# Float32 projections to r, k and v, replaced by three products of rounded parts

## The chip, the cores and the metric

The kernel runs on one core of a Trainium2 chip. The metric is the device time of one execution in microseconds, as the median over runs. TensorE (PE) multiplies matrices into PSUM, VectorE (DVE) and ScalarE (ACT) work on SBUF and PSUM, GpSimd (POOL) and SyncE (SP) here mostly issue DMAs. Each engine follows its own program in order; they meet at semaphores.

## The reference

Two layers of a streaming encoder run over 1024 prompt frames and 64 frames of a sample; with padding that is T = 1092 columns of 1024 features. Layer 1 starts with RWKV-7 time mixing. What matters here is its beginning:

```python
xr, xw, xk, xv, xa, xg = (x + xx * mu[n] for n in range(6))   # xx: the frame before minus this one
r = xr @ w_r
k = xk @ w_k
v = xv @ w_v
logw = -jax.nn.softplus(-(w0 + jnp.tanh(xw @ w1) @ w2).astype(f32)) - 0.5
a = jax.nn.sigmoid((a0 + (xa @ a1) @ a2).astype(f32))
g = jax.nn.sigmoid(xg @ g1) @ g2
...
xs = tuple(t.transpose(1, 0, 2, 3) for t in (r_h, w_h, k_h, v_h, kk, b_h))
S_fin, o = lax.scan(step, wkv_prev.astype(f32), xs)
```

r, k and v are products of 1024 x 1024 weights with 1088 frames each. They are stored by head pair and go into a recurrence over chunks of 64 frames. All data are float32.

## The kernel before, in words

Activations lie feature-major: 8 tiles of 128 features by 1092 columns. A *unit* is one tile of 128 output features: all eight k-tiles by three column groups of 364, so 24 products into three PSUM banks. Two sets of banks alternate (`read0`, `read1`). Weights come by SP in chunks of 512 KB, one to a unit, into four slots of `W`, three units ahead.

There are two forms of unit. `unit` (line 404) multiplies float32 operands as they are: 24 matmuls. `split_unit` (line 425) works on rounded parts. A weight chunk w has an upper part wh (w cast to the rounded type float32r) and a rest wl = w - wh, an activation x has xh and xl, and the unit sums wh xh + wh xl + wl xh: 72 matmuls (line 443). DVE makes wh by a cast and wl in place by a subtraction (`split_chunk`, lines 1477 and 1478); ACT makes xh by a copy that rounds (lines 1026 and 1031), DVE xl by a subtraction (lines 1493 and 1504). The rounded names (`H_r`, `B_r`, `W_r`, `TM_r`) are the same memory as `H`, `B`, `W`, `TM`. Nearly all large products have the split form already; r, k and v have the plain one.

At the start of layer 1, `H` holds the residual and stays in SBUF; `A` holds the normed input. For each of six mixtures ACT scales a tile into `TM` (`mix`, line 1228), and DVE adds the shifted tile into one of two blocks of `B` (tiles 0 to 7 and 8 to 15, line 1436). The order is w, a, g, r, k, v. The first three go through two small products each (`lora`, lines 735 to 754). Then PE runs 8 units for r and 8 for k (`dense8`, line 495). ACT copies each unit from PSUM into one of four staging tiles of `B` (line 1253), and POOL stores it to DRAM (`keep`).

v is computed in a loop over eight head pairs (PE line 766, ACT 1280, DVE 1798, POOL 2132). For each pair POOL has loaded r, k, w and a from DRAM (`load_pair`, line 2126). ACT scales and squares the key (1285, 1288), PE sums the squares over a head, runs the pair's v unit, and sums the bonus products (`sums`, line 457); ACT copies both results out (1312, 1315). DVE meanwhile forms the factors of the recurrence: a first step on `a` (1803), the product with k (1806), the bonus product, a scan and the final products (1829 to 1837). POOL stores v, the bonus sums and the factors, then loads the pair after the next. What follows is the recurrence, whose chunks POOL loads (`load_chunk`, line 2164, `double_chunk`, lines 2170 and 2171).

Of the kernel before, what the change touches and what calls it, by code (L numbers as in the profile page):

```python
# [139 lines left out]
def build_trunk(nc, I, O, stop=99):  # L140
    ctx = ExitStack()
    with ctx:
# [11 lines left out]
        with ExitStack() as rounded:  # L154
# [35 lines left out]
                 "down": (DWr[:, 0, :], DWr[:, 1, :])}  # L190
# [97 lines left out]
        def c3(ap):  # L288
            return ap.rearrange("p (c n) -> p c n", c=NCH)

        def pset(s):
            return ps[:, NCH * s:NCH * s + NCH, 0:CH]
# [19 lines left out]
                 "xn_ready", "xn_tmp", "xv0", "xv1", "xv2", "xv3", "xs0", "xs1", "xs2", "xs3", "key_sq", "rk_ready", "gn_in", "dev_sq",  # L312
# [84 lines left out]
        def _(pe):  # L397
# [598 lines left out]
        def _(act):  # L996
# [225 lines left out]
            def mix(n):  # L1222

                for kt in range(KT):
# [29 lines left out]

            def hidden(slot, rows, func):
# [15 lines left out]
            stage()  # L1271
            mix(2)
            stage()
            mix(3)
            stage()
# [4 lines left out]
            with t.loop(2, l_in0=2 * 64, l_in1=2 * 64, act_p=16, dve_p=8, mm_done=12, read0=6, read1=6, key_scaled=4,  # L1280
                        key_sq=4, key_max=4, key_log=4, xs0=16, xs1=16, xs2=16, xs3=16) as i:
                for u in range(4):
# [27 lines left out]
                    act.wait_ge(S[f"xs{u}"], t.val(f"xs{u}"))  # L1310
                    t.up(f"xs{u}", 16)
                    nc.scalar.activation(c3(B[:, 18 + u, :]), pset(s), ACT.Copy).then_inc(S[f"read{s}"], 1)
# [114 lines left out]
        def _(dve):  # L1427
# [344 lines left out]
            for order, n in enumerate((1, 4, 5, 0, 2, 3)):  # L1772
                b = order % 2
                if order >= 2:
                    dve.wait_ge(S["mm_done"], read_by[order - 2])
                for kt in range(KT):
                    j = t.n.get("xn_tmp", 0) % 2
                    dve.wait_ge(S["xn_tmp"], t.up("xn_tmp"))
                    stt(B[:, 8 * b + kt, 1:T], A[:, kt, 0:T - 1], vec[:, V["mu0"] + n, kt:kt + 1], TM[:, j, 1:T],
                        ALU.mult, ALU.add).then_inc(S["xn_ready"], 1)  # L1780
                    t.up("xn_ready")
            t.skip(43)
# [15 lines left out]
            with t.loop(2, l_in0=2 * 64, l_in1=2 * 64, act_p=16, dve_p=8, mm_done=12, read0=6, read1=6, dve_step=12,  # L1798
                        key_rn=4, key_scaled=4, rk_ready=4, rn_used=4, pair_stored=4, sum_stored=4, pair_done=4) as i:
                for u in range(4):  # L1800
# [3 lines left out]
                                                 kab[:, bass.ds(pair, 1)], ALU.mult, ALU.add))  # L1804
                    dve.wait_ge(S["key_scaled"], t.up("key_scaled"))
# [172 lines left out]
            for i in range(NPAIR):  # L1978
# [11 lines left out]
                nc.vector.tensor_tensor(out, dev, gate, ALU.mult).then_inc(S["gn_ready"], 1)  # L1990
            channel_mixer(1)
# [3 lines left out]
        def _(pool):  # L1995
# [101 lines left out]

            pool.wait_ge(S["shift_in"], 1)
# [19 lines left out]
            for name in "rk":  # L2118
                keep(name)
# [12 lines left out]
            for i in range(NPAIR):  # L2132
# [3 lines left out]
                j = i % 4  # L2136
                pool.dma_start(d_v[i, :, 0:SEQ], B[:, 18 + j, P0:P0 + SEQ]).then_inc(S[f"xv{j}"], 16)
                pool.dma_start(d_v[i, :, SEQ:SEQ + C], B[:, 18 + j, S0:T]).then_inc(S[f"xs{j}"], 16)
                t.up(f"xs{j}", 16)
# [12 lines left out]
            for j in range(4):  # L2152
                pool.wait_ge(S[f"xs{j}"], t.val(f"xs{j}"))
                pool.wait_ge(S[f"xv{j}"], 32)
# [199 lines left out]
```

## Time and profile before

| what | us |
|---|---|
| runs: median of 3 (lowest, highest) | 4127.3 (4125.62, 4127.95) |
| profiled execution: its time | 4123.89 |
| profiled execution: its span | 4122.3 |
| PE busy in it | 3726.8 (90%) |
| DVE busy, ACT busy | 1461.3, 831.4 |

The span runs from the first to the last instruction of the one execution that was profiled; the profile's times count from its start. A row of a timeline merges like instructions and gives the idle time of the engine before them with what released it. A float32 matmul leaves two records, a rounded one one.

### The profile page before, as it was taken

How to read it: one execution, taken by the hardware profiler on the slowest of the kernel's cores; microseconds unless marked ns; L12 is line 12 of the kernel's file. 1: busy time of each engine (PE TensorE's matmuls, PEld its weight loads, DVE VectorE, ACT ScalarE, POOL GpSimd, SP SyncE). 2: the span in 40 equal slices, each digit the busy share in tenths (PEclk: the TensorE clock that was granted, in tenths of full speed). 3: DMA queues.
4: the chain of work that ended last, by engine and by line, in shares of the span. 5: the costliest groups of instructions: out<-in, count | busy, mean ns of one | idle time of the engine just before them, and what ended most of it. 6: DMA issues, size and time to landing. Idle time of an engine off the chain costs nothing.

```text
span 4122.3 us, 64833 instructions
## 1 busy us (share of the span) xinstructions
PE 3726.8 (90%) x27922; PEld 3201.6 (78%) x27922; DVE 1461.3 (35%) x1951; ACT 831.4 (20%) x1107; POOL 203.2 (5%) x345
## 2 busy tenths in 40 slices
PE   7998899899999998878998868889797999999977
PEld 4996337789999998754564537878496999999967
DVE  3123544342212223432211645555635222222352
ACT  2000232210000001223311423333322000000021
POOL 0001000000000000000000211111100000000000
PEclk9998999999999999986999989999999999999989
DMA  2212002111121131002222652211311112112211
GB/s 87 73 53 85 21 21 76 70 45 41 46 83 48 46 124 47 29 21 107 96 74 103 258 187 54 53 45 52 139 42 69 46 36 73 62 46 87 77 37 69
DMA packets 75064, 291.43 MB, mean 71 GB/s; under 512 B 9368, under 2 KB 11688, under 8 KB 71128
## 3 DMA queue, kind: packets, MB, share of 16 engines
q0 software_dynamic: 36528, 165.56, 11.1%
q1 hardware_dynamic: 38336, 122.87, 9.6%
q8 instruction: 167, 2.74, 0.3%
q14 instruction: 33, 0.27, 0.0%
HBM read 211.77 MB, written 76.62 MB: 70 GB/s over the span
## 4 chain that ended last, share of the span: by engine, by line
PE 72%; DVE 8%; ACT 2%; issue 2%; DMA 1%; POOL 0%; DVEq 0%; ACTq 0%; POOLq 0%
PE ps L443 47%; PE ps L417 11%; DVE A L1436 2%; PE ps L836 2%; PE ps L845 2%; DVE B L1436 1%; PE ps L750 1%; PE ps L457 1%; DVE H L1517 1%; PE ps L796 1%; DVE A_r L1493 1%; PE ps L475 1%; DVE B L1900 1%; PE ps L859 1%; PE ps L823 1%
## 5 line engine op out<-in xcount | busy, mean ns | idle before, releaser
L443 PE MATMUL ps<-A_r,TM_r 128*128 128x364 f32 x2736 | 605.3, 329 | 0.0
L443 PE MATMUL ps<-H_r,W_r 128*128 128x364 f32 (+1 forms) x2616 | 576.3, 328 | 0.0
L443 PE MATMUL ps<-H_r,TM_r 128*128 128x364 f32 x2352 | 520.8, 329 | 19.0 <-DVE A_r L1493 19.0
L417 PE MATMUL ps<-B,W 128*128 128x364 f32 (+1 forms) x1488 | 469.7, 477 | 24.9 <-DVE B L1436 24.9
L443 PEld LDWEIGHTS ps<-A_r,TM_r 128*128 128x128 f32 x2736 | 476.0, 189 | 0.0
L443 PEld LDWEIGHTS ps<-H_r,W_r 128*128 128x128 f32 (+1 forms) x2616 | 453.5, 187 | 1.8
L417 PEld LDWEIGHTS ps<-B,W 128*128 128x128 f32 (+1 forms) x1488 | 282.5, 190 | 207.6 <-issue 28.7
L443 PEld LDWEIGHTS ps<-H_r,TM_r 128*128 128x128 f32 x2352 | 408.0, 188 | 23.7 <-issue 14.5
L443 PE MATMUL ps<-B_r,DW_r 128*128 128x364 f32 x2112 | 408.8, 329 | 0.0
L443 PE MATMUL ps<-B_r,W_r 128*128 128x364 f32 x1824 | 404.6, 330 | 0.0
L443 PEld LDWEIGHTS ps<-B_r,DW_r 128*128 128x128 f32 x2112 | 358.8, 188 | 0.0
L443 PEld LDWEIGHTS ps<-B_r,W_r 128*128 128x128 f32 x1824 | 319.3, 189 | 0.0
L1695 DVE TENSOR_TENSOR TM<-ps,TM 128x1092 f32<-128x1092 f32 x44 | 57.0, 1296 | 444.1 <-PE ps L443 444.1
L1477 DVE CAST TM_r<-W 128x1024 fp32r<-128x1024 f32 x114 | 78.7, 690 | 321.7 <-PE ps L443 301.9
L443 PE MATMUL ps<-B_r 128*128 128x364 f32 x768 | 152.2, 334 | 14.3 <-DVE B_r L1504 14.3
L1169 ACT ACTIVATE B_r<-TM 128x1092 f32 (+1 forms) x44 | 49.2, 1118 | 542.6 <-DVEq L1697 542.6
L475 PE MATMUL ps<-TM,cst 128*128 128x364 f32 x288 | 107.9, 533 | 55.0 <-ACT TM L1004 55.0
L443 PEld LDWEIGHTS ps<-B_r 128*128 128x128 f32 x768 | 133.8, 192 | 15.5 <-issue 15.5
L1436 DVE SCALAR_TENSOR_TENSOR B<-A,vec,TM 128x1091 f32<-128x1091 f32 x48 | 62.9, 1352 | 225.0 <-ACT TM L1228 224.9
L1478 DVE TENSOR_TENSOR W_r<-W,TM_r 128x1024 fp32r<-128x1024 f32 x114 | 139.7, 1226 | 3.9
L475 PEld LDWEIGHTS ps<-TM,cst 128*128 128x128 f32 x288 | 60.3, 216 | 103.9 <-issue 65.9
L836 PE MATMUL ps<-B 64*64 64x64 f32 x2720 | 116.3, 224 | 25.9 <-issue 12.0
(279 smaller groups left out, 4146.4 us busy)
## 6 DMA issues: line engine op xcount, KB each, us to landing
W<-in_wgu SPq DMA_DIRECT2D x88, 512.0 KB, 3.6
W<-in_wdown SPq DMA_DIRECT2D x32, 384.0 KB, 3.1
W<-in_wrkv SPq DMA_DIRECT2D x24, 512.0 KB, 3.7
W<-in_wdown SPq DMA_DIRECT2D x32, 320.0 KB, 2.9
d_h<-H POOLq DMA_DIRECT2D x16, 546.0 KB, 3.0
d_y<-TM POOLq DMA_DIRECT2D x16, 546.0 KB, 3.6
A<-d_y POOLq DMA_DIRECT2D x16, 546.0 KB, 7.8
H<-d_h POOLq DMA_DIRECT2D x2, 4368.0 KB, 22.7
```

Source lines behind the costliest of these rows:

```text
L417: ins = nc.tensor.matmul(ps[0:cols, NCH * s + c, 0:CH], W[0:rows, slot, j * cols:(j + 1) * cols], xs[n][0:rows, c * CH:(c + 1) * CH], star ...
L443: ins = nc.tensor.matmul(ps[0:cols, NCH * s + c, 0:CH], w[:, j * cols:(j + 1) * cols], x[k1][:, c * CH:(c + 1) * CH], start=(k1 == 0 and n ...
L457: ins = nc.tensor.matmul(ps[:, NCH * s + c, 0:CH], lhs, x[:, c * CH:(c + 1) * CH], start=True, stop=True)
L475: ins = nc.tensor.matmul(ps[:, NCH * s + c, 0:CH], k("ones"), TM[:, j % 2, c * CH:(c + 1) * CH], start=(j == 0), stop=(j == KT - 1))
L750: ins = nc.tensor.matmul(ps[:, NCH * s + c, 0:CH], W[0:rows, slot, m * P:(m + 1) * P], out[0:rows, c * CH:(c + 1) * CH], start=True, stop= ...
L836: ins = nc.tensor.matmul(ps[r, g, C * a:C * a + C], AB[c % 2][r, p, :], Ms[c % 2][r, p, :], start=True, stop=True)
L845: ins = nc.tensor.matmul(ps[r, g, 256 + C * a:256 + C * a + C], MT[r, p, :], Y[r, p, :], start=True, stop=True)
L1169: nc.scalar.activation(hi, TM[:, j, :], ACT.Copy).then_inc(S["mid_hi"], 1)
L1436: return nc.vector.scalar_tensor_tensor(out=out, in0=in0, scalar=scalar, in1=in1, op0=op0, op1=op1)
L1477: step(nc.vector.tensor_copy(wh, w))
L1478: nc.vector.tensor_tensor(Wr[:, slot, 0:n], w, wh, ALU.subtract).then_inc(S["wl_ready"], 1)
L1695: nc.vector.tensor_tensor(c3(TM[:, j, :]), pset(s), c3(TM[:, j, :]), ALU.mult).then_inc(S[f"read{s}"], 1)
```

## The change

The 24 units of r, k and v become split units. The upper parts of the mixtures go into `H_r`, that is, into the residual's memory. POOL therefore stores the residual to DRAM as soon as it is complete (`d_h`, semaphore `hs_out`), and loads it back in the first chunks of the recurrence (`hs_in`). The rests xl stay in the mixture's block of `B`.

There is one `H_r` for three mixtures: the upper part of the next is written after PE's last unit on the one before. Weights are split by DVE (`split_weights`), each chunk at the earliest when the unit before the last has ended; upper parts of weights alternate between two tiles (of `TM` for r and k, of `B` for v). Since two of the four staging tiles hold those of v, the copies of r, k and v alternate between two tiles. In the loop over pairs DVE splits one chunk per pair.

```diff
-                 "down": (DWr[:, 0, :], DWr[:, 1, :])}
+                 "down": (DWr[:, 0, :], DWr[:, 1, :]),
+                 "rkv": (TMr[:, 2, 0:KT * P], TMr[:, 3, 0:KT * P]),
+                 "value": (Br[:, 20, 0:KT * P], Br[:, 21, 0:KT * P])}
...
+            xh = [Hr[:, j, :] for j in range(KT)]
+            xlow = [[Br[:, 8 * b + j, :] for j in range(KT)] for b in range(2)]
+            enter(t, "rkv")
             for n in range(2):
-                pe.wait_ge(S["xn_ready"], t.up("xn_ready", KT))
-                xs = X[(n + 1) % 2]
-                dense8(KT)
-
-            pe.wait_ge(S["xn_ready"], t.up("xn_ready", KT))
-            xs = X[1]
-            with t.loop(2, mm_done=12, read0=6, read1=6, key_sq=4, rk_ready=4, chunk=4, w_used=4, w0=16, w1=16, w2=16, w3=16):
+                t.up("xn_ready", KT)
+                split_units(KT, xh, xlow[(n + 1) % 2])
+
+            t.up("xn_ready", KT)
+            enter(t, "value")
+            pe.wait_ge(S["xl_ready"], t.up("xl_ready", KT))
+            with t.loop(2, mm_done=12, read0=6, read1=6, key_sq=4, rk_ready=4, chunk=4, w_used=4, w0=16, w1=16, w2=16, w3=16,
+                        wl_ready=4, wh=4):
                 for u in range(4):
                     pe.wait_ge(S["key_sq"], t.up("key_sq"))
                     sums(k("pair"), TM[:, 1, :])
-                    unit([KT], xs)
+                    split_unit(xh, xlow[1])
                     pe.wait_ge(S["rk_ready"], t.up("rk_ready"))
                     sums(k("pair"), TM[:, 2, :])
 
...
+
+            def staged(n, bufs):
+
+                j = n % bufs
+                s, mm, rd = t.unit()
+                act.wait_ge(S["mm_done"], mm)
+                act.wait_ge(S[f"xs{j}"], t.val(f"xs{j}"))
+                t.up(f"xs{j}", 16)
+                nc.scalar.activation(c3(B[:, 18 + j, :]), pset(s), ACT.Copy).then_inc(S[f"read{s}"], 1)
+
+            def upper_mixed(b, kt):
+
+                act.wait_ge(S["xn_ready"], t.val("xn_tmp", kt + 1 - KT))
...
             mix(0)
-            stage()
+            act.wait_ge(S["hs_out"], 16)
+            for n in range(KT):
+                staged(n, 4)
+                upper_mixed(1, n)
             mix(2)
-            stage()
-            mix(3)
-            stage()
+            for n in range(KT):
+                staged(n, 2)
+            for n in range(KT):
+                upper_mixed(0, n)
+            for n in range(KT):
+                if n < 2:
+                    mix(3, 4 * n, 4 * n + 4)
+                staged(n, 2)
+            for n in range(KT):
+                upper_mixed(1, n)
 
 
             log_and_exp()
             act.wait_ge(S["xn_ready"], t.val("xn_tmp"))
             with t.loop(2, l_in0=2 * 64, l_in1=2 * 64, act_p=16, dve_p=8, mm_done=12, read0=6, read1=6, key_scaled=4,
...
-                    nc.scalar.activation(c3(B[:, 18 + u, :]), pset(s), ACT.Copy).then_inc(S[f"read{s}"], 1)
+                    act.wait_ge(S[f"xs{u % 2}"], t.val(f"xs{u % 2}"))
+                    t.up(f"xs{u % 2}", 32)
+                    nc.scalar.activation(c3(B[:, 18 + u % 2, :]), pset(s), ACT.Copy).then_inc(S[f"read{s}"], 1)
...
-            for order, n in enumerate((1, 4, 5, 0, 2, 3)):
-                b = order % 2
-                if order >= 2:
+            def mix(order, n, k0=0, k1=KT):
+
...
+
+                for kt in range(KT):
+                    dve.wait_ge(S["xh_ready"], t.up("xh_ready"))
+                    nc.vector.tensor_tensor(Br[:, 8 * b + kt, :], B[:, 8 * b + kt, :], Hr[:, kt, :],
+                                            ALU.subtract).then_inc(S["xl_ready"], 1)
+                    t.up("xl_ready")
+
+            def split_weights(done):
+
+                slot, landed = t.chunk()
+                if done:
+                    dve.wait_ge(S["mm_done"], done)
+                dve.wait_ge(S[f"w{slot}"], landed)
+                w, wh = W[:, slot, 0:KT * P], wh_of(t)
+                step(nc.vector.tensor_copy(wh, w))
+                nc.vector.tensor_tensor(Wr[:, slot, 0:KT * P], w, wh, ALU.subtract).then_inc(S["wl_ready"], 1)
+                t.up("wl_ready")
+
+            t.n["chunk"] = t.n["w0"] = t.n["w1"] = t.n["w2"] = t.n["w3"] = 0
+            t.skip_chunks(CHUNKS[1] - 4 * KT)
+            enter(t, "rkv")
+            mix(0, 1)
+            mix(1, 4)
+            mix(2, 5)
+            mix(3, 0)
+            split_weights(0)
+            lower_mixed(1)
+            split_weights(0)
+            mix(4, 2)
+            for m in range(2, KT + 1):
+                split_weights(mm0 + 27 + m - 1)
+            lower_mixed(0)
+            split_weights(mm0 + 27 + KT)
+            dve.wait_ge(S["mm_done"], read_by[3])
+            step(nc.vector.memset(B[:, 8:16, 0:1], 0.0))
+            mix(5, 3, 0, 4)
+            split_weights(mm0 + 27 + KT + 1)
+            mix(5, 3, 4, 8)
+            for m in range(KT + 3, 2 * KT):
+                split_weights(mm0 + 27 + m - 1)
+            enter(t, "value")
+            dve.wait_ge(S["xs2"], 96)
+            dve.wait_ge(S["xs3"], 96)
+            lower_mixed(1)
...
                 for u in range(4):
                     pair, key, L = i * 4 + u, key2[u % 2], Lb[u % 2]
                     dve.wait_ge(S[f"l_in{u % 2}"], t.up(f"l_in{u % 2}", 64))
                     step(nc.vector.tensor_scalar(tmpA, L["a"], vec[:, V["ka"], bass.ds(pair, 1)],
                                                  kab[:, bass.ds(pair, 1)], ALU.mult, ALU.add))
+                    split_weights(0)
                     dve.wait_ge(S["key_scaled"], t.up("key_scaled"))
...
+            dve.wait_ge(S["hs_in"], 16)
             channel_mixer(1)
...
+            pool.wait_ge(S["h_ready"], 24)
+            pool.dma_start(d_h, H[:, :, :]).then_inc(S["hs_out"], 16)
             pool.wait_ge(S["shift_in"], 1)
...
+            pool.wait_ge(S["hs_out"], 16)
+            pool.dma_start(H[:, :, :], d_h).then_inc(S["hs_in"], 16)
             with t.loop(3, u_done=8, tok_done=8, zi0=96, zi1=96) as i:
```

Left out: counts in the loops' headers, and POOL's stores of r, k and v, which go over two staging tiles instead of four.

DVE from the mixture of w to the loop over pairs, before (1436: six mixtures of eight tiles; the memsets prepare the scan):

```order
L1436 SCALAR_TENSOR_TENSOR B<-A,vec,TM 128x1091 x48
L1786 MEMSET B 128x1092
L1787 MEMSET B 128x16
L1788 MEMSET B 128x1
L111 UNCONDITIONAL_BRANCH
```

and the same place now, up to the third weight chunk of r (1466: mixtures; 1828, 1829: `split_weights`; 1817: `lower_mixed`):

```order
L1466 SCALAR_TENSOR_TENSOR B<-A,vec,TM 128x1091 x32
L1828 CAST TM_r<-W 128x1024
L1829 TENSOR_TENSOR W_r<-W,TM_r 128x1024
L1817 TENSOR_TENSOR B_r<-B,H_r 128x1092 x8
L1828 CAST TM_r<-W 128x1024
L1829 TENSOR_TENSOR W_r<-W,TM_r 128x1024
L1466 SCALAR_TENSOR_TENSOR B<-A,vec,TM 128x1091 x8
L1828 CAST TM_r<-W 128x1024
```

The mixtures no longer stand in one run: after those of w, a, g and r come the first weights and the rests of r, then the mixture of k, and from there a pair of splitting instructions for each unit.

ACT now, from r's mixture to the loop over pairs (1234: `mix`; 1268: `staged`, a copy out of PSUM; 1273: `upper_mixed`); the copy and the upper part before the "..." stand eight times in turn:

```order
L1234 ACTIVATE TM<-A,mub 128x1092 x8
L1268 ACTIVATE B<-ps 128x1092
L1273 ACTIVATE H_r<-B 128x1092
...
L1234 ACTIVATE TM<-A,mub 128x1092 x8
L1268 ACTIVATE B<-ps 128x1092 x8
L1273 ACTIVATE H_r<-B 128x1092 x8
L1234 ACTIVATE TM<-A,mub 128x1092 x4
L1268 ACTIVATE B<-ps 128x1092
L1234 ACTIVATE TM<-A,mub 128x1092 x4
L1268 ACTIVATE B<-ps 128x1092 x7
L1273 ACTIVATE H_r<-B 128x1092 x8
```

Before, only mixtures and copies alternated here. Upper parts of r stand between the copies of g; those of k stand behind the last copy of r, those of v behind the last copy of k.

DVE at the start of a pair, before:

```order
L1803 TENSOR_SCALAR A<-B,vec,kab 128x1092
L1433 ISA
L1805 REGISTER_ALU
L1806 TENSOR_TENSOR B<-A,B 128x1092
L1433 REGISTER_ALU
```

and now (1880 is 1803, 1884 is 1806):

```order
L1880 TENSOR_SCALAR A<-B,vec,kab 128x1092
L1463 ISA
L1826 REGISTER_ALU
L1828 CAST B_r<-W 128x1024
L1463 REGISTER_ALU
L1829 TENSOR_TENSOR W_r<-W,B_r 128x1024
L1883 REGISTER_ALU
L1884 TENSOR_TENSOR B<-A,B 128x1092
```

The cast and the subtraction stand between the pair's first step and the product that waits for ACT's scaled key.

## Rows read from the trace of the kernel before

**Rows 1.** Page, head: the whole profiled execution.

```profile
span 4122.3 us, 64833 instructions
```

**Rows 2.** Stretch table of the r and k units: busy per engine, clock, DMA share.

```profile
1990.96:2226.00 235.04, 235.04 (x769) 145.73 (x767) 20.97 (x16) 36.12 (x32) 9.05 (x17) 1.00 0.22 78
```

**Rows 3.** Chain of waits, one rounded unit: start us, us, what.

```profile
1690.24 11.95 PE ps L443 x72
```

**Rows 4.** PE's timeline, g units to v units: start us, us, what, [idle before <-releaser].

```profile
1977.51 13.62 PE L750 MATMUL ps<-B,W 128*128 128x364 f32 x36 [7.34 <-ACT B L1253]
...
1990.96 235.04 PE L417 MATMUL ps<-B,W 128*128 128x364 f32 x768
...
2243.52 4.00 PE L457 MATMUL ps<-TM,cst 128*128 128x364 f32 x6 [17.52 <-ACT TM L1288]
...
2315.57 2.86 PE L457 MATMUL ps<-TM,cst 128*128 128x364 f32 x6 [3.48 <-ACT TM L1288]
...
2318.23 15.82 PE L417 MATMUL ps<-B,W 128*128 128x364 f32 x48
...
2408.96 3.76 PE L457 MATMUL ps<-TM,cst 128*128 128x364 f32 x6 [3.48 <-ACT TM L1288]
```

**Rows 5.** Splitting instructions by line: min/median/max ns, first and last start.

```profile
L1031 ACT ACTIVATE B_r<-B x16: 1096/1098/1113, 689.7 to 2999.4; 128x1092 fp32r<-128x1092 f32 x16
...
L1477 DVE CAST TM_r<-W x114: 685/690/695, 58.3 to 4072.7; 128x1024 fp32r<-128x1024 f32 x114
...
L1478 DVE TENSOR_TENSOR W_r<-W,TM_r x114: 1224/1226/1228, 59.0 to 4073.4; 128x1024 fp32r<-128x1024 f32 x114
...
L1504 DVE TENSOR_TENSOR B_r<-B,B_r x16: 1285/1289/1291, 691.6 to 3002.5; 128x1092 fp32r<-128x1092 f32 x16
```

**Rows 6.** PE's timeline after the longer idle before the output projection.

```profile
2995.53 2.16 PE L443 MATMUL ps<-B_r 128*128 128x364 f32 x6 [10.18 <-DVE B_r L1504]
...
3000.36 1.16 PE L443 MATMUL ps<-B_r 128*128 128x364 f32 x6
...
3001.86 1.16 PE L443 MATMUL ps<-B_r 128*128 128x364 f32 x6
```

**Rows 7.** ACT's timeline around the g units.

```profile
1976.39 2.03 ACT L1253 ACTIVATE B<-ps 128x1092 f32<-128x1092 f32 x2
...
1981.55 1.08 ACT L1253 ACTIVATE B<-ps 128x1092 f32<-128x1092 f32 x1 [3.13 <-PE ps L750]
```

**Rows 8.** ACT's timeline from the last k unit to the first pair.

```profile
2226.04 1.08 ACT L1253 ACTIVATE B<-ps 128x1092 f32<-128x1092 f32 x1 [13.60 <-PE ps L417]
...
2241.04 1.21 ACT L1285 ACTIVATE A<-B,vec 128x1092 f32<-128x1092 f32 x1 [12.62 <-DMA B<-d_a]
```

**Rows 9.** DVE's timeline in one pair of the v loop.

```profile
2314.33 1.29 DVE L1806 TENSOR_TENSOR B<-A,B 128x1092 f32<-128x1092 f32 x1 [4.70 <-ACT A L1285]
...
2316.85 1.35 DVE L1436 SCALAR_TENSOR_TENSOR TM<-B,vec 128x1092 f32<-128x1092 f32 x1 [1.23 <-POOLq L2144]
...
2330.24 1.35 DVE L1436 SCALAR_TENSOR_TENSOR A<-A,B 128x1024 f32<-128x1024 f32 x2
...
2332.35 0.85 DVE L1803 TENSOR_SCALAR A<-B,vec,kab 128x1092 f32<-128x1092 f32 x1 [0.75 <-DMA B<-d_a]
```

**Rows 10.** Stretch table of single pairs of the v loop.

```profile
2314.60:2338.30 23.70, 20.30 (x60) 12.12 (x60) 16.11 (x17) 10.84 (x13) 4.77 (x9) 0.93 0.68 258
...
2385.90:2408.00 22.10, 18.62 (x60) 11.32 (x60) 16.19 (x17) 11.01 (x13) 4.76 (x9) 1.00 0.72 276
```

**Rows 11.** POOL's DMA issues for the next pair, by line.

```profile
L2126 POOL DMA_DIRECT2D B<-d_a x8: 528/528/531, 2233.8 to 2391.5; - x8
```

**Rows 12.** Page, DMA issues: the residual's load: KB each, us to landing.

```profile
H<-d_h POOLq DMA_DIRECT2D x2, 4368.0 KB, 22.7
```

**Rows 13.** POOL's timeline at the start of the recurrence.

```profile
2484.75 0.62 POOL L2171 COPY B<-B 128x512 f32<-128x512 f32 x1
...
2515.32 0.88 POOL L2164 DMA_DIRECT2D B<-d_bk  x1 [5.87 <-PE ps L823]
```

More of the change, by code:

```diff
@@ L311, in build_trunk @@
                  "pt_done", "pt_read", "o_done", "o_read", "ot_done", "ot_read", "bias_in0", "bias_in1", "kv_in0", "kv_in1", "attn_pair",
[L312 removed]
+                 "xn_ready", "xn_tmp", "hs_out", "hs_in", "xs0", "xs1", "xs2", "xs3", "key_sq", "rk_ready", "gn_in", "dev_sq",
                  "b_out", "key_scaled", "sum_out", "pair_done", "pair_stored", "sum_stored", "rn_used", "key_max", "key_log", "key_rn", "l_in0", "l_in1", "gn_in0", "gn_in1", "mean_in", "gn_used", "shift_in", "conv_out",
@@ L1220, in _, with mix @@
             act.wait_ge(S["dve_p"], t.up("dve_p"))
-            def mix(n):
-                for kt in range(KT):
+            def mix(n, k0=0, k1=KT):
+                for kt in range(k0, k1):
                     j = t.n.get("xn_tmp", 0) % 2
@@ L1253, in stage @@
                         nc.scalar.activation(c3(B[:, 18 + j, :]), pset(s), func, **kw).then_inc(S[f"read{s}"], 1)
+            def staged(n, bufs):
[7 more added lines that the diff above has]
+                act.wait_ge(S["xn_ready"], t.val("xn_tmp", kt + 1 - KT))
+                nc.scalar.activation(Hr[:, kt, :], B[:, 8 * b + kt, :], ACT.Copy).then_inc(S["xh_ready"], 1)
             def hidden(slot, rows, func):
@@ L1280, in _ @@
             with t.loop(2, l_in0=2 * 64, l_in1=2 * 64, act_p=16, dve_p=8, mm_done=12, read0=6, read1=6, key_scaled=4,
-                        key_sq=4, key_max=4, key_log=4, xs0=16, xs1=16, xs2=16, xs3=16) as i:
+                        key_sq=4, key_max=4, key_log=4, xs0=64, xs1=64) as i:
                 for u in range(4):
@@ L1771, in _ @@
             dve.wait_ge(S["dve_step"], t.up("dve_step"))
-            for order, n in enumerate((1, 4, 5, 0, 2, 3)):
-                b = order % 2
-                if order >= 2:
+            def mix(order, n, k0=0, k1=KT):
+                if order >= 2 and k0 == 0:
                     dve.wait_ge(S["mm_done"], read_by[order - 2])
-                for kt in range(KT):
+                for kt in range(k0, k1):
                     j = t.n.get("xn_tmp", 0) % 2
                     dve.wait_ge(S["xn_tmp"], t.up("xn_tmp"))
-                    stt(B[:, 8 * b + kt, 1:T], A[:, kt, 0:T - 1], vec[:, V["mu0"] + n, kt:kt + 1], TM[:, j, 1:T],
+                    stt(B[:, 8 * (order % 2) + kt, 1:T], A[:, kt, 0:T - 1], vec[:, V["mu0"] + n, kt:kt + 1], TM[:, j, 1:T],
@@ L1780, in _, with lower_mixed @@
                         ALU.mult, ALU.add).then_inc(S["xn_ready"], 1)
                     t.up("xn_ready")
+            def lower_mixed(b):
+                for kt in range(KT):
[12 more added lines that the diff above has]
+                t.up("wl_ready")
@@ L1796, in tokens @@
                 return ap[:, P0:P0 + SEQ].rearrange("p (c n) -> p c n", n=C), ap[:, S0:T]
-            with t.loop(2, l_in0=2 * 64, l_in1=2 * 64, act_p=16, dve_p=8, mm_done=12, read0=6, read1=6, dve_step=12,
-                        key_rn=4, key_scaled=4, rk_ready=4, rn_used=4, pair_stored=4, sum_stored=4, pair_done=4) as i:
+            with t.loop(2, l_in0=2 * 64, l_in1=2 * 64, act_p=16, dve_p=8, mm_done=12, read0=6, read1=6, dve_step=16,
+                        key_rn=4, key_scaled=4, rk_ready=4, rn_used=4, pair_stored=4, sum_stored=4, pair_done=4,
+                        chunk=4, w0=16, w1=16, w2=16, w3=16, wl_ready=4, wh=4) as i:
                 for u in range(4):
@@ L2118, in _ @@
             for name in "rk":
-                keep(name)
+                with t.loop(4, mm_done=2, read0=1, read1=1, xs0=16, xs1=16) as i:
+                    for j in range(2):
+                        s, mm, rd = t.unit()
+                        pool.wait_ge(S[f"read{s}"], rd)
+                        pool.sem_inc(S["held"], 1)
+                        pool.dma_start(d_x[name][bass.ds(i * 2 + j, 1)].rearrange("a p n -> (a p) n"),
+                                       B[:, 18 + j, :]).then_inc(S[f"xs{j}"], 16)
+                        t.up(f"xs{j}", 16)
             for j in range(4):
@@ L2135, in _ @@
                 pool.wait_ge(S[f"read{s}"], rd)
-                j = i % 4
-                pool.dma_start(d_v[i, :, 0:SEQ], B[:, 18 + j, P0:P0 + SEQ]).then_inc(S[f"xv{j}"], 16)
+                j = i % 2
+                pool.dma_start(d_v[i, :, 0:SEQ], B[:, 18 + j, P0:P0 + SEQ]).then_inc(S[f"xs{j}"], 16)
                 pool.dma_start(d_v[i, :, SEQ:SEQ + C], B[:, 18 + j, S0:T]).then_inc(S[f"xs{j}"], 16)
-                t.up(f"xs{j}", 16)
+                t.up(f"xs{j}", 32)
                 s, mm, rd = t.unit()
```

3 lines of the change are left out of this document (removed).

## The prediction

> **What bounds the kernel now.** I read the head of the page first: a span of 4122.3 us [rows 1]. The profiled execution took 4123.9 us, so 1.6 us lie outside the span; the median of the runs shown is 4127.3, 3.4 us above it. The sum is made against 4123.9, and 3.4 is added at the end.
>
> Then I looked for what the change touches. The stretch table shows that PE was busy for all of the 235.04 us of the r and k units, at a granted clock of 1.00, the 2.4 GHz level, while DVE worked for 20.97 us and ACT for 36.12 [rows 2]. PE alone bounds this stretch, and DVE has room. PE's timeline gives its content: 768 records, two to a float32 matmul, so 384 matmuls in 16 units of 24; 235.04 / 16 = 14.69 us a unit, 612 ns a matmul [rows 4]. The chain of waits has the price of the other form in the same kernel: a unit of 72 rounded matmuls takes 11.95 us, 166 ns each [rows 3]. That unit is the one at line 443, with the same 128x364 shape. Three products for 498 ns stand against one for 612.
>
> The v units stand in a loop over eight head pairs. A pair there is a serial ring: PE's sum (2.86 us), PE's unit (15.82 with some time at the lower clock level), PE's second sum, two ACT steps, and PE's next sum, before which PE sat idle 3.48 us for ACT [rows 4]. From the first sum at 2243.52 to the eighth at 2408.96 are seven pairs of 23.63 us.
>
> **The change part by part.** *Units.* 24 units fall from 14.69 to 11.95, 2.74 us each: 16 x 2.74 = 43.8 us for r and k, which stand back to back on PE, and 8 x 2.74 = 21.9 us for v, if the ring closes no sooner elsewhere.
>
> By the Trainium skill (TensorE: Matmul & The Clock Gate, "Wait — 56ns, not 53.3ns?") warm matmuls follow each other after their columns at 2.4 GHz plus about 2.5 ns. For 364 columns that is an estimate of 154 ns, a unit of 11.1 us, and 20 us more gain over 24 units, so about 4048. The trace does not agree for this form, 166 ns in [rows 3], and the measurement decides; the sum stays with 11.95.
>
> *Start of r.* ACT now makes one upper part (1.10 us, line 1031 [rows 5]) between two copies of g units (1.08 [rows 7]), 2.18 us a unit. Its third g copy started at 1981.55, after a wait for PE [rows 7]; two copies and two uppers from 1976.39 end at 1980.75, so this start stands. The seventh copy then starts at 1981.55 + 4 x 2.18 = 1990.3 and ends at 1991.4; it frees the PSUM set of the first r unit, which began at 1990.96 [rows 4]. Cost 0.6 us. The k-tiles of r come every 2.18 us from long before, the last at about 1996, and PE asks for its eighth some 10 us after its start. Bounds: nothing, and 4.9 us if PE had to wait for all eight; I take 0.6.
>
> *From r to k.* There is one block for upper parts, so k's cannot be written until PE has ended the last r unit. PE then waits for ACT's copy (1.08 [rows 7]), the first upper (1.10) and the first subtraction (1.29 [rows 5]), and three hand-overs. One is about 0.13 us: the sum of a pair began at 2315.57 [rows 4], 1.24 after the ACT step before it, which takes about 1.1 like line 1031's and starts when line 1806 does, at 2314.33 [rows 9]. So 3.47 + 0.4 = 3.9 us. Further tiles come each 1.29 us, faster than the 1.50 that PE takes for nine matmuls [rows 6]. After an idle PE starts at the lower clock level: after 10.18 us idle two tiles took 4.83 us instead of 3.0, 1.8 lost [rows 6]; in the v loop, idle 3.48 us, a pair takes 23.7 us at a mean clock of 0.93, and one at 1.00 took 22.1, so 1.6 lost [rows 10]. The second idle is nearer in length: 1.6. Bounds 0 and 1.8. Together 5.5 us.
>
> *Supply of weights.* Each unit asks DVE for a cast (0.69) and a subtraction (1.23 [rows 5]), 1.92 us of 11.95, made a unit ahead; 16 x 1.92 + 16 x 1.29 of new work beside 20.97 in some 198 us. It is hidden by PE's units. The thinnest cover is the second k unit: its weights are split behind eight subtractions of k, that is 2.5 + 8 x 1.29 + 1.92 = 14.7 us after the end of r, and the first k unit ends at 3.9 + 1.6 + 11.95 = 17.5. Without these 2.8 us PE waits by what is missing.
>
> *From k to v.* PE sat idle 17.52 us here already [rows 4], for the store of the last k tile and the loads of the first pair, which ended ACT's wait of 12.62 us at 2241.04 [rows 8]. The eight uppers of v start after the copy at 2226.04 + 1.08 and end 8 x 1.10 later, 2235.9; the last subtraction ends at 2237.2. The table load and the memset that stand there still fit. Cost 0.
>
> *The v loop.* DVE gets 1.92 us, put between its first step on a pair (line 1803) and the product at line 1806. Counted from 1806 at 2314.33: the last products end at 2331.59, +17.3; 1803 waited 0.75 for the pair's load and began at +18.0 [rows 9]. With 0.85 for it and 1.92 for the split DVE is ready at +20.8 to +21.0. The ring closes at 23.63 - 2.74 = 20.89. That is level; but the next step waited 1.23 us for POOL's store of the bonus sums in any case [rows 9], so DVE may be a microsecond late for nothing. ACT asks for the load 1.2 us before 1806, at +19.7, and it landed at +18.0. Both covers shrink to 1 to 2 us; none is gone. I take the whole 21.9. From the other side: if the clock came back, DVE's own round of 17.3 + 0.85 + 1.92 = 20.0 us is the floor, 8 x 3.6 = 29 us. At worst the loop keeps its 23.63 and gains nothing.
>
> The casts meet a rule of the Trainium skill (SBUF — State Buffer, "SBUF: two separate sides"): a VectorE copy in a two-port mode locks GpSimd out and holds up the descriptors of DMAs that it issues. POOL issues this loop's stores and loads; its issue took 528 to 531 ns in all eight pairs [rows 11], with no cast beside it. By the rule a cast of 0.69 could hold each pair's chain once, 5.5 us in all, 4074 instead of 4068; it runs 2 us or more away from the loads, so I leave it out.
>
> *The residual.* Its store is issued before layer 1's norm, and the two first lora products lie between it and its first need. The reload takes 22.7 us [rows 12]. POOL reaches it after the copy at 2484.75, so it would end at 2508.1, in the old time; the queue's next load came at 2515.32 [rows 13]. Cost 0; if nothing hid it, 22.7.
>
> *Sum:* -43.8 + 0.6 + 5.5 - 21.9 = -59.6 us; 4123.9 - 59.6 = 4064.3; with 3.4, **4068 us** for the median.
>
> **The rivals.** *A new bound in the loop.* The load of the pair or DVE's round takes the place of PE's unit. For it: the DMA engines were 0.68 busy in a pair [rows 10], and the same bytes in 20.9 us make 0.77, so the load may land later than +18.0; beyond +19.7 each microsecond is a microsecond of the period. Against: stores and loads start from the same event as before, so they keep their places to each other. The loop would gain between 0 and about 13 us: 4077 to 4090.
>
> *More than the sum.* The idle before k does not lower the clock, and the loop's clock recovers, so that DVE's 20.0 us is the period: -1.6 and -7 more, 4059; if the first k tile also came without ACT's copy in front, 4055.
>
> *Slower: the clock in the rounded units.* The changed program has one idle more, at k, and the loop's idle of 3.48 us stands in a shorter pair. If the granted clock stayed at 1.2 GHz for a share f of the 24 units, each such unit would take 23.9 us. The gain is gone at 24 x 11.95 x f = 59, f = 0.21, and the kernel is 0.2% slower from f = 0.24; at f = 0.3 it is 4154. Against: the r and k units ran at 1.00 although an idle of 7.34 us stood shortly before [rows 4], and the rounded units of [rows 3] hold 166 ns, possible only at 2.4 GHz.
>
> *It does not do what it says:* the units cost PE as much as before (operands that are written shortly before could be read slower), and only the 6 us of gaps come in: about 4134, no change.
>
> **How the numbers follow.** The measurement tells apart about 0.2%, 8 us. Forecast: 0.70, own range 4060 to 4077. New bound in the loop: 0.17, 4077 to 4090. More: 0.07, 4047 to 4060. No effect: 0.03. Slower: 0.03. So faster 0.94, same 0.03, slower 0.03. The range reaches into both neighbours, 4055 to 4088.
>
> **What would show it.** Right: 16 runs of 72 rounded matmuls at 11.95 to 12.0 us; one idle of about 4 us between the eighth and ninth; PE's idle before the first pair still near 17.5; periods of 20.9 in the loop, with 1803 still waiting for the load and 1806 for ACT or hardly at all. Wrong: idles before units ended by DVE's subtraction of weights; periods above 21.5 with ACT waiting for the pair's load; a granted clock under 0.95 in the r and k stretch; PE waiting at the start of the recurrence for POOL's copies.

## The result and the profile after

The changed kernel takes 4101.9 us in the median (4098.2 to 4107.4) against 4127.3: a ratio of 0.9935, 95% interval 0.9922 to 0.9948. It is faster, by 25 us where 59 were forecast, and lies outside the range given. The profiled execution is the longest of its three, 4107.4 us.

First the page's head, then the stretch table (from:to, us, busy us and instructions of PE, PE's weight loads, DVE, ACT and POOL, granted clock, DMA share, GB/s) for r and k. They answer [rows 1, 2].

```profile
span 4105.5 us, 66070 instructions
```

```profile
1991.65:2087.41 95.76, 95.75 (x576) 95.44 (x575) 28.23 (x27) 19.62 (x18) 4.80 (x9) 1.00 0.30 101
2090.99:2188.51 97.52, 97.50 (x576) 97.20 (x576) 31.98 (x30) 22.28 (x21) 3.73 (x7) 0.98 0.25 87
```

The span fell by 16.8 us. The sixteen units are there as forecast: 95.76 / 8 = 11.97 us each for r. The chain of waits (start us, us, what) shows the hand-over from r to k, and PE's timeline (start us, us, what, [idle before <-releaser]) the loop over head pairs and the start of the recurrence; they answer [rows 3, 4].

```profile
1991.65 95.76 PE ps L445 x576
...
2087.43 1.08 ACT B L1268
2088.52 1.01 ACT H_r L1273
...
2089.55 1.31 DVE B_r L1817
...
2090.99 97.52 PE ps L445 x576
```

```profile
1978.03 13.62 PE L752 MATMUL ps<-B,W 128*128 128x364 f32 x36 [7.34 <-ACT B L1268]
1991.40 0.76 PE L445 MATMUL ps<-H_r,TM_r 128*128 128x364 f32 x3
...
2206.21 4.00 PE L459 MATMUL ps<-TM,cst 128*128 128x364 f32 x6 [17.71 <-ACT TM L1318]
...
2355.49 4.00 PE L459 MATMUL ps<-TM,cst 128*128 128x364 f32 x6 [3.48 <-ACT TM L1318]
...
2401.10 6.98 PE L533 MATMUL ps<-cst 128*128 128x512 f32 x10 [26.75 <-POOL B L2258]
```

The last row is the five matmuls (ten records) that raise the clock ahead of the recurrence. They began at 2457.41 in the kernel before and begin at 2401.10 now: 56.3 us of the 59.6 are there at this point. The same table over the recurrence, from these matmuls to the eleven of the same kind behind it, shows where they go: the kernel before, then the changed one.

```profile
2457.40:2911.50 454.10, 393.88 (x10155) 358.35 (x10155) 239.48 (x540) 163.04 (x400) 67.95 (x93) 0.96 0.18 48
```

```profile
2401.10:2890.60 489.50, 413.37 (x10155) 374.91 (x10155) 241.85 (x540) 161.98 (x400) 68.99 (x95) 0.91 0.19 54
```

The same 10,155 matmul records take 35.4 us more: 19.5 us of PE's busy time, at a granted clock of 0.91 instead of 0.96, and 15.9 us of idle (60.2 to 76.1). Behind the recurrence another 4.1 us are lost, and -56.3 + 35.4 + 4.1 = -16.8. No line of PE's code in the recurrence was touched. What PE waits for there (line <- releaser: us in all, times, longest), before and after:

```profile
PE ps L796 <- DVE B L1900: 24.7, 16, 2.5
PE ps L836 <- issue: 12.0, 10, 3.7
```

```profile
PE ps L842 <- issue: 27.5, 12, 3.5
...
PE ps L901 <- issue: 9.9, 4, 2.8
PE ps L802 <- DVE B L1978: 7.8, 8, 2.5
```

(Lines 796 and 836 of before are 802 and 842 now.) "Issue" is a wait for nothing that the profile shows. It has taken the place of the wait for DVE. Of the 12.0 us before, 7.2 stand at the two jumps back of PE's loop; there the changed kernel loses 6.5 of its 27.5, so the rest has grown from 4.8 to 21.0. PE's timeline shows where one stands, first before, then after:

```profile
2521.09 0.66 PE L845 MATMUL ps<-TM 64*64 64x64 f32 x16
2523.27 1.16 PE L796 MATMUL ps<-B 64*128 64x128 f32 x16 [1.52 <-DVE B L1900]
```

```profile
2463.78 0.41 PE L842 MATMUL ps<-B 64*64 64x64 f32 x6
2466.52 0.56 PE L842 MATMUL ps<-B 64*64 64x64 f32 x10 [2.32 <-issue]
...
2467.53 2.08 PE L802 MATMUL ps<-B 64*128 64x128 f32 x16
```

PE stops after six of a group's sixteen records, that is inside its eight float32 matmuls, whose waits all stand ahead of the first. So it lacks no operand; what it lacks is instructions, as the packets show below. The stop swallows the wait for DVE, and the next matmuls run at the lower clock level (2.08 us for what takes 1.16). The page has a DMA queue named instruction, 173 packets of 16,384 bytes; in this stretch PE's next packet began 2463.86 in the trace, 7.5 us after the last at 2456.40, where 4 to 6 us are common. POOL's loads for a later chunk stand in between. Its timeline, and the DMA view of 2457.8 to 2465.8 (busy tenths and GB/s in 40 slices, then the queues: packets, MB, share):

```profile
2458.29 0.89 POOL L2251 DMA_DIRECT2D B<-d_bk  x1 [5.85 <-PE ps L829]
...
2460.05 0.88 POOL L2251 DMA_DIRECT2D B<-d_v  x1
```

```profile
DMA  0000000000599537989999999999999998632010
GB/s 0 0 0 0 0 0 0 0 0 0 82 143 123 82 123 205 389 348 451 348 307 287 287 307 287 287 287 287 287 307 348 266 266 205 143 62 41 0 20 0
...
q0 software_dynamic: 364, 1.30, 59.9%
q8 instruction: 1, 0.02, 1.0%
```

The DMA engines are full from about 2461 to 2464.5, and the one packet of instructions comes at the end of that. By its record in the trace it has landed at 2465.09, and PE goes on 1.43 us later, at 2466.52.

That holds for nearly every such stop. Take the idle of PE, jumps back left out, that ends with no releaser, from 20 us into the recurrence on. In the changed kernel it is 46.3 us, and 45.2 of them end 1.1 to 1.8 us behind the landing of an instruction packet; in the kernel before it is 10.1 us, 7.9 of them behind a packet. Both kernels take 87 packets in the recurrence, one for 117 records of matmuls. Their number has not changed, only what PE has to wait for at them.

### The profile page after: what moved, and what is told of

Its sections match the earlier page's. It is cut to its first block, busy times and chain, and to the rows that moved or that the text cites. A ratio compares the mean times of both kernels' runs of the same rounds, so it can differ in the third digit from the quotient of the medians.

```text
span 4105.5 us, 66070 instructions
## 1 busy us (share of the span) xinstructions
PE 3695.8 (90%) x28498; PEld 3297.6 (80%) x28498; DVE 1538.2 (37%) x2024; ACT 853.8 (21%) x1131; POOL 207.6 (5%) x347
## 4 chain that ended last, share of the span: by engine, by line
PE 72%; DVE 7%; issue 2%; ACT 2%; DMA 1%; POOL 0%; DVEq 0%; ACTq 0%; POOLq 0%
PE ps L445 54%; PE ps L419 3%; DVE A L1466 2%; PE ps L851 2%; PE ps L842 2%; PE ps L459 1%; PE ps L752 1%; DVE B L1466 1%; PE ps L802 1%; DVE H L1547 1%; DVE A_r L1523 1%; PE ps L891 1%; PE ps L477 1%; PE ps L868 1%; PE ps L865 1%
## 5 line engine op out<-in xcount | busy, mean ns | idle before, releaser
L445 PE MATMUL ps<-H_r,W_r 128*128 128x364 f32 (+1 forms) x3192 | 704.9, 329 | 0.0
L445 PE MATMUL ps<-H_r,TM_r 128*128 128x364 f32 x2736 | 606.5, 330 | 21.7 <-DVE A_r L1523 18.1
L445 PEld LDWEIGHTS ps<-H_r,W_r 128*128 128x128 f32 (+1 forms) x3192 | 555.4, 188 | 1.8
L445 PEld LDWEIGHTS ps<-H_r,TM_r 128*128 128x128 f32 x2736 | 475.5, 189 | 26.5 <-issue 18.3
L445 PE MATMUL ps<-B_r 128*128 128x364 f32 x960 | 196.2, 335 | 13.9 <-DVE B_r L1534 13.9
L445 PE MATMUL ps<-B_r,TM_r 128*128 128x364 f32 x768 | 176.5, 338 | 17.9 <-DVE A_r L1523 17.9
L445 PEld LDWEIGHTS ps<-B_r 128*128 128x128 f32 x960 | 169.0, 194 | 15.1 <-issue 15.1
L445 PEld LDWEIGHTS ps<-B_r,TM_r 128*128 128x128 f32 x768 | 135.1, 191 | 24.7 <-issue 13.8
L842 PE MATMUL ps<-B 64*64 64x64 f32 x2720 | 116.8, 226 | 39.2 <-issue 27.5
L1952 DVE COPY_PREDICATED B<-lvl,ps 128x256 f32<-128x256 uint8 x170 | 75.3, 443 | 178.8 <-PE ps L851 177.9
```

Source lines behind the costliest of these rows:

```text
L445: ins = nc.tensor.matmul(ps[0:cols, NCH * s + c, 0:CH], w[:, j * cols:(j + 1) * cols], x[k1][:, c * CH:(c + 1) * CH], start=(k1 == 0 and n ...
L842: ins = nc.tensor.matmul(ps[r, g, C * a:C * a + C], AB[c % 2][r, p, :], Ms[c % 2][r, p, :], start=True, stop=True)
L1952: nc.vector.copy_predicated(Ms[c % 2][:, 4 * g:4 * g + 4, :], four(lvl[:, l + 1, :]), half_of(g, 256)).then_inc(S["m_ready"], 1)
```

## The theories

*A, the place of the code.* PE's instructions arrive in packets. The change puts 1440 more rounded and 288 fewer float32 matmuls into PE's code ahead of the recurrence (a loop's body counts once). With two and four instructions each, and 2 others, that is 2880 - 1152 + 2 = 1730 more, 194 above a multiple of 256, the number of instructions that theory A takes for a packet. So the seams between packets fall on other matmuls of every chunk. A1: a seam is dear where its packet is asked for beside POOL's loads and no wait of PE covers it. A2: a packet takes its time whatever else moves. *B, the residual's reload* disturbs the recurrence. *C, the clock* falls there by itself. *D,* the new code costs it in some other way.

## Experiments on the place of the code

The padding is one line ahead of the wait in which PE sat idle for 26.75 us:

```diff
+            for _ in range(62):
+                pe.sem_inc(S["held"], 1)
             pe.wait_ge(S["st_ready"], 1)
```

Expected of 62:

> The changed kernel with 62 semaphore increments on PE ahead of the recurrence, in the 26.75 us in which PE waits there for POOL. Theory A (place of the code): the change put some 1730 more instructions on PE ahead of the recurrence, which is 194 above a multiple of 256; PE's instructions come in packets of 16,384 bytes, one for every 121 or so matmul records, so the seams between packets lie at other matmuls of each chunk than before, and PE now stops there for 2 us in each of 17 chunks. 62 more bring the seams back to where they were: the recurrence, from the matmuls that raise the clock to the first store of the state, 486.8 us now, goes back to 452 to 456, and the kernel to 4066 to 4073. Theory B (the residual's reload disturbs the recurrence): nothing changes, 4098 to 4107. Theory C (the clock falls in the recurrence by itself, because of what ran before): nothing changes, 4098 to 4107.

Of 256, 128, 94, 190 and 30:

> A control for the padding: 256 semaphore increments at the same place, still inside PE's wait of 26.75 us. Theory A: the seams lie as in the changed kernel without padding, so the recurrence takes 484 to 489 us and the kernel 4098 to 4107. If padding of any length helped (by delaying PE, or by what it does to the clock), it would fall to 4066 to 4073 as with 62. Theories B and C: 4098 to 4107.

> 128 semaphore increments at the same place: half a packet, some 61 matmul records. Theory A: the seams lie at a third place; they go past more of a chunk's matmuls, so the time of the recurrence is neither bound to 487 nor to 453, I expect 445 to 490 and say only that it moves by more than 5 us against the changed kernel without padding (4066 to 4095 for the kernel). Theories B and C: 4098 to 4107.

> 94 semaphore increments ahead of the recurrence, between the place that gave 4070 (62) and the one that gave 4093 (128). Theory A, no more than that a seam's place decides: between 4065 and 4095, and stops of PE at a line that differs from those of 62 and of 128. Theories B and C would have it at 4098 to 4107.

> 190 semaphore increments on PE ahead of the recurrence: 30.0 us at 158 ns, 3.3 us more than PE's wait there, so a start 3 us late. The seams lie some 30 matmul records later than in the changed kernel without padding, if 256 instructions are one packet. Theory A: between 4070 and 4105, with stops at other lines than 842. If the seams repeat every 256 instructions, the time lies between those of 128 (4093) and 256 (4101, of which 14 are its late start), so 4085 to 4100.

> 30 semaphore increments: the seams lie some 15 matmul records earlier in a chunk than without padding, half way to the place that 62 gave. Theory A: between 4070 and 4102, I say 4086; stops still in line 842's groups in part of the chunks. Theories B and C: 4098 to 4107.

Measured (medians of four runs, of ten for 190 and three for none; ratio to the kernel before, run beside it, with its 95% interval; recurrence and PE busy from the stretch table as above; the last column has the idle behind instruction packets, counted as above, and how many of these stops are longer than 1 us):

| padding | median us | ratio | recurrence us | PE busy in it | stops us (over 1 us) |
|---|---|---|---|---|---|
| 0 | 4101.9 | 0.9935 (0.9922 to 0.9948) | 489.5 | 413.4 | 45.2 (17) |
| 30 | 4097.7 | 0.9933 (0.9915 to 0.9952) | 474.7 | 404.9 | 22.3 (5) |
| 62 | 4070.2 | 0.9859 (0.9842 to 0.9876) | 451.1 | 392.2 | 6.3 (2) |
| 94 | 4079.7 | 0.9886 (0.9869 to 0.9902) | 461.8 | 398.3 | 11.9 (3) |
| 128 | 4092.8 | 0.9916 (0.9899 to 0.9933) | 479.2 | 402.5 | 23.3 (5) |
| 190 | 4122.4 | 0.9989 (0.9978 to 1.0000) | 499.3 | 419.9 | 27.4 (10) |
| 256 | 4100.7 | 0.9942 (0.9925 to 0.9959) | 469.1 | 401.6 | 32.8 (13) |

Idle instructions, 62 of them, bring back 32 us, and 190 of them eat nearly all that the change had won. With 62 the waits of the recurrence read as those of the kernel before:

```profile
PE ps L802 <- DVE B L1980: 25.0, 16, 2.5
PE ps L842 <- issue: 11.2, 8, 3.8
```

With 190 the stops stand at other lines:

```profile
PE ps L533 <- issue: 30.6, 1, 30.6
PE ps L851 <- issue: 17.0, 12, 3.0
...
PE ps L802 <- issue: 14.6, 8, 3.4
```

B and C fall as the cause of these 32 us: neither has a reason why a few increments in an idle wait should matter. With 30, half way to 62 in the code, the time stays near that of none: no halving of the way halves the loss. The last column does not put the recurrences in order by itself: 190 has fewer stops than 0 and the longest recurrence, with the most PE busy time, at a granted clock of 0.91.

Three expectations were missed. With 94, PE's longest waits were to stand at a line other than with 62; they stand at line 842 in both (14.5 us with 94). The time with 190 was to lie between 4085 and 4100: I had drawn a line between two neighbours, and the curve has no such line, since what decides is which group of matmuls the seam cuts. The first row above shows that its increments outlasted the wait, 30.6 us against 26.75. The control with 256 has its stops at lines 842 and 901 as without padding, one of them on the very record of the 2.32 us stop above:

```profile
2475.85 0.41 PE L842 MATMUL ps<-B 64*64 64x64 f32 x6
2478.58 0.75 PE L842 MATMUL ps<-B 64*64 64x64 f32 x10 [2.32 <-issue]
```

So 256 increments move the seams by a whole packet. It has the total of the kernel without padding too, but by two errors that cancel: its increments took 40.6 us, which starts the recurrence 13.9 us late, and the recurrence took 469.1 us, not 484 to 489. The seams' place gives the place of the stops; what they cost at one place still differs between versions (469 to 490 us). The medians say so too: without its late start 256 would be 11 to 15 us faster than 0. Why stays open.

The other direction, in the kernel before, with 194 of the same increments:

> The kernel before, its r, k and v units untouched, with 194 semaphore increments on PE ahead of the recurrence, which puts the seams between the packets of PE's instructions where they lie in the changed kernel. One increment took 158 ns in the run with 256 (40.6 us in all), so 194 take 30.7 us, 2.5 us more than PE's wait of 28.18 there. Theory A (place of the code): PE now stops in the middle of line 836's 16 matmuls, as the changed kernel does at line 842, and the recurrence goes from 454 to between 469 and 490 us (what the runs with the same seams took); the kernel to 4145 to 4165 (454 to 469 or 490, and 2.5). Theory D (the stops come from the new code itself, its reload or its split units): 4125 to 4132, 2.5 us from the late start and nothing else.

It took 4148.2 us, ratio 1.0046 (1.0030 to 1.0062), slower by 18, of which 2.9 are the late start (31.1 us against 28.2). The recurrence took 470.6 us instead of 454.1, with old units and no reload. Its waits:

```profile
PE ps L531 <- issue: 31.1, 1, 31.1
PE ps L836 <- issue: 28.3, 14, 4.7
...
PE ps L895 <- issue: 6.2, 3, 2.4
PE ps L796 <- DVE B L1902: 5.7, 7, 2.5
```

The stops stand at the lines (836, 895) that are 842 and 901 in the changed kernel, and at the same record:

```profile
2528.22 0.41 PE L836 MATMUL ps<-B 64*64 64x64 f32 x6
2530.68 0.59 PE L836 MATMUL ps<-B 64*64 64x64 f32 x10 [2.04 <-issue]
```

(The sixteen in the expectation are records, of eight matmuls.) The stops behind packets grow from 7.9 us to 31.7. D falls as the cause of the stops: they need none of the new code. In size this run shows 16.5 of the 35.4 us, as the changed kernel does with the same seams at 256 (15.0).

## Experiments on the loads and the reload

Smaller loads:

```diff
-                    pool.dma_start(dst, src.rearrange("a p n -> p a n")[:, :, cols]).then_inc(S[f"zi{c % 2}"], 16)
+                    pool.dma_start(dst[:, 0:pairs, :], src.rearrange("a p n -> p a n")[:, 0:pairs, cols]).then_inc(S[f"zi{c % 2}"], 16)
...
-                    load_chunk(c + 3, at + 3)
+                    load_chunk(c + 3, at + 3, NPAIR if c == 0 else 1)
```

> The changed kernel, no padding, with the chunk loads of POOL in the recurrence cut to one head pair of eight, in three of four chunks; what it leaves out is the data of seven pairs in those chunks. PE's code is the same. Theory A1 (at the bad seams the packet of instructions waits behind POOL's loads on the DMA engines): the stops of 2 us at line 842 go in the chunks with small loads, the recurrence falls from 486.8 to 450 to 462, and the kernel to 4066 to 4080. Theory A2 (a packet takes its time whatever else the DMA engines do; it is only where the seam lies that counts): the stops stay, the recurrence at 469 to 490, the kernel at 4085 to 4105.

Measured: 4077.1 us, ratio 0.9880 (0.9864 to 0.9897); the recurrence 457.5. One run holds both cases. PE's timeline at the same place of two neighbouring chunks, then POOL's loads of the two, full ones (0.90 us to issue) and small ones (0.56):

```profile
2572.45 0.56 PE L842 MATMUL ps<-B 64*64 64x64 f32 x10 [2.04 <-issue]
...
2599.03 1.16 PE L802 MATMUL ps<-B 64*128 64x128 f32 x16 [1.31 <-DVE B L1978]
```

```profile
2564.64 0.90 POOL L2251 DMA_DIRECT2D B<-d_bk  x1 [5.72 <-PE ps L829]
...
2591.00 0.56 POOL L2251 DMA_DIRECT2D B<-d_bk  x1 [5.46 <-PE ps L829]
```

Behind full loads PE stops after six of sixteen records as in the changed kernel; behind small ones, with the same code, it does not stop, and waits for DVE as in the kernel before. The other chunks agree: after six records of line 842 PE stops for 0.89, 2.04 and 1.16 us in the three chunks of the loop with full loads, and from there on no stop behind a packet is over 0.8 us elsewhere. (The longest behind a packet, 4.05 us, stands ahead of them, beside the reload.) Then the full loads, only later:

```diff
+                    for _ in range(14):
+                        pool.sem_inc(S["held"], 1)
                     load_chunk(c + 3, at + 3)
```

> The changed kernel, no padding on PE (its seams stay at the bad place), with 14 semaphore increments on POOL between its wait for the token-major products and the three loads of a chunk: some 2.2 us at the 158 ns that one took on PE. The loads are wanted a chunk later, so PE does not wait for them. Theory A1 (a packet of instructions that PE asks for just behind the loads waits for them): the packet that stops line 842 now, wanted some 5 us after the one at 2456.40 and begun only at 2463.86, goes ahead of the loads' bytes; the stops at line 842 go in most chunks and the kernel comes to 4066 to 4085. Theory A2 (the seam's place alone): 4092 to 4105.

> The same with 30 increments, some 4.7 us. Theory A1: the packet of line 842 is free, but the next one, some 5 us later, now stands behind the loads; whether that stops PE depends on whether a wait for DVE covers it: stops at a line that comes after line 842's group, and a kernel between 4066 and 4105. Theory A2: 4092 to 4105 with stops at lines 842 and 901 as without.

Measured: 4077.6 us, 0.9884 (0.9860 to 0.9908), and 4081.4, 0.9895 (0.9877 to 0.9914); the recurrences 467.5 and 463.9. An increment on POOL takes less than I had taken from PE: the wait ahead of the loads grew from 5.85 us to 6.95 and 7.82, so the delays were 1.1 and 2.0 us. The first is enough. PE's timeline at the place of the 2.32 us stop above:

```profile
2465.91 0.41 PE L842 MATMUL ps<-B 64*64 64x64 f32 x6
2466.72 0.56 PE L842 MATMUL ps<-B 64*64 64x64 f32 x10 [0.40 <-issue]
...
2468.58 1.16 PE L802 MATMUL ps<-B 64*128 64x128 f32 x16 [0.78 <-DVE B L1978]
```

The seam is where it was, after the sixth record, and it costs 0.40 us. Over the recurrence the stops longer than 1 us that end behind a packet fall from 17 to 7 and to 2 (45.2 us of stops to 25.7 and 15.9). A2 falls, A1 holds. The later delay did not move the long stops to a line behind 842 as I had half expected; perhaps 2.0 us is too short for that, and a delay of 4.7 was not run.

The reload, alone and beside the padding of 62:

```diff
-            pool.wait_ge(S["hs_out"], 16)
-            pool.dma_start(H[:, :, :], d_h).then_inc(S["hs_in"], 16)
             with t.loop(3, u_done=8, tok_done=8, zi0=96, zi1=96) as i:
...
+            pool.wait_ge(S["hs_out"], 16)
+            pool.dma_start(H[:, :, :], d_h).then_inc(S["hs_in"], 16)
             pool.wait_ge(S["c_in"], 2 + 2 * NCHUNK)
```

> The changed kernel with the residual's reload moved from the start of the recurrence to behind its last chunk, on the same queue, ahead of the first store of the state. PE's code is the same to the instruction. Theory A: the recurrence still takes 482 to 489 us (at most a few us of the first chunk, whose loads the reload's 22.7 us could hold up), the kernel 4095 to 4110. Theory B: the recurrence goes back to 452 to 456 and the kernel to 4066 to 4075. Theory C: 4098 to 4107.

> 62 semaphore increments and the residual's reload behind the recurrence, both. If the reload costs the 10 us that the median of its own experiment fell by, whatever the seams: 4057 to 4063. If those 10 us were the seams' stops falling otherwise (theory A): as with 62 alone, 4065 to 4073.

Alone it gave 4091.6 us, 0.9919 (0.9895 to 0.9942), with a recurrence of 471.1: below what A expected, far from B's 4066 to 4075. With 62 it gave 4077.9, 0.9876 (0.9859 to 0.9894), above both ranges that were expected and no better than 4070.2 without the move. The recurrence took 452.5 against 451.1, so the rest of that difference lies outside it and is not explained. With the seams at a good place the reload costs the recurrence nothing that these runs show. At the bad place it adds to the stop that it meets. The first stop, at line 842 in the first chunk, was 3.50 us with the reload on the queues and 1.03 without; but the reload at its new place met the last stop, at line 851, which rose from 1.23 to 3.82. The two cancel, so most of the 10 us is something else, and stays open.

## Why the prediction was wrong, step by step

*Units:* right. 11.97 us for r against 11.95. *Start of r:* r began at 1991.40, 0.44 us later than before; 0.6 forecast. *From r to k:* PE idle from 2087.41 to 2090.99, 3.58 us (3.9 forecast), and k takes 97.52 - 95.76 = 1.76 us more than r while the clock comes back (1.6 forecast): 5.3 of 5.5. *From k to v:* 17.71 us against 17.52 [rows 4].

*The v loop:* the mechanism right, the size 3.5 us short. From the first sum to the eighth (2206.21, 2355.49) are seven periods of 21.33 us, 20.89 forecast: 8 x (23.63 - 21.33) = 18.4 of 21.9. Five periods are 20.99 to 21.03, the other two 21.93 and 22.35, with a first sum of 4.00 us at the lower clock level. DVE's round has become level with the ring, as worked out from [rows 9]: its step on the pair's load waits for it, the split follows, and then the product hardly waits for ACT (0 to 0.42 us).

```profile
2246.33 0.85 DVE L1880 TENSOR_SCALAR A<-B,vec,kab 128x1092 f32<-128x1092 f32 x1 [1.41 <-DMA B<-d_a]
2247.21 0.69 DVE L1828 CAST B_r<-W 128x1024 fp32r<-128x1024 f32 x1
2247.94 1.23 DVE L1829 TENSOR_TENSOR W_r<-W,B_r 128x1024 fp32r<-128x1024 f32 x1
2249.08 1.29 DVE L1884 TENSOR_TENSOR B<-A,B 128x1092 f32<-128x1092 f32 x1
```

The rule of the Trainium skill that the prediction weighed and left out (SBUF — State Buffer, "SBUF: two separate sides": a two-port copy on VectorE locks GpSimd out) does show in this loop, though not at the loads that the prediction looked at. Those keep the price of [rows 11], 2 us or more away from the casts. The stores of v meet them (the first of their two lines before, then after, and the loads after):

```profile
L2137 POOL DMA_DIRECT2D d_v<-B x8: 532/537/537, 2264.2 to 2428.8; - x8
```

```profile
L2225 POOL DMA_DIRECT2D d_v<-B x8: 532/627/1029, 2224.3 to 2373.9; - x8
```

```profile
L2214 POOL DMA_DIRECT2D B<-d_a x8: 528/528/531, 2196.8 to 2339.0; - x8
```

Eleven issues of stores took 0.59 to 1.03 us instead of 0.53 to 0.55. Each of them overlaps the step at line 1880 or a cast, and each ends 0.11 to 0.12 us behind that instruction. The ring pays little for it: five of the seven periods lie within 0.14 us of the forecast.

*The residual:* right at 0 where the seams lie well, as the pair of experiments with 62 shows; where they lie badly, the stop that it meets grew by some 2.5 us. PE waited 26.75 us for POOL's copies ahead of the recurrence, less than the 28.18 of before.

*The sum:* here it failed. It went from the start of the recurrence to the end of the kernel as if code that is not edited kept its time, "4123.9 - 59.6 = 4064.3". The term that was missing, put at nothing without a word, is the place of PE's code: the recurrence took 489.5 us instead of 454.1, +35.4 in the profiled execution. No rival had it either; the price for a slower outcome was sought in the new units. With the seams put back, by 62 increments, the kernel takes 4070.2 us (4064.9 to 4072.9) against the 4068 forecast. Against the kernel before in the same series, 4126.9, that is 56.7 us of the 59.6, and the 2.9 that are missing are about the 3.5 of the v loop: the sum for the edited part holds once the recurrence keeps its time (451.1 us in that run, 454.1 before). That version also beats both kernels, and is the one to keep.

## What to carry to other kernels

A change in the number of PE's instructions moved all its later code against the packets in which that code arrives. In this loop of short matmuls beside heavy loads, padding alone was worth from -32 to +20 us (3.9 of the 20 are a late start), as much as the change itself. So when a stage that was not edited changes its time, look for idle marked "issue" in the middle of a group whose waits stand ahead of it, see whether an instruction packet lands just before it ends, and compare the same kernel at two or three paddings in an idle wait before a small gain or loss is believed. Two things mended a bad place here: a padding of the right length (62), and the colliding loads a microsecond later (4077.6 us).

## What the runs showed of the hardware

PE's code comes in packets of 16,384 bytes, one for 117 matmul records in the recurrence; where PE had to wait for one, it went on 1.1 to 1.8 us after the packet had landed. A packet beside POOL's loads began 7.5 us after the one before and stopped PE for 2.32 us. With the loads 1.1 us later the stop was 0.40 us, and in the run with small loads there was none behind them. The Trainium skill (Runtime: NRT & Kernel Launch, "Instruction fetch mechanics") says that code streams in blocks of 256 instructions over a DMA queue of its own and that a crossing is mostly hidden. The trace agrees with the blocks, since 256 increments left the seam on its record, and not with hidden: 45.2 us of stops behind packets in the recurrence after, 7.9 before. A stop can cost more than its length: behind that of 2.32 us the next groups ran at the lower clock level, and 19.5 of the 35.4 us are PE's longer busy time. It need not: behind the stop of 2.04 us in the run with small loads line 802 took its 1.16 us. A semaphore increment that waits for nothing took 0.16 us on PE (40.6 us for 256) and, as an estimate from the longer wait, about 0.07 on POOL (2.0 us for 30). Eleven of POOL's DMA issues beside a cast, or beside the step at line 1880, on DVE ended 0.11 to 0.12 us behind it.
